# A two-layer fp32 transformer trunk: overlapped halves of the QK projection, layer 1's attention written out, and an earlier first weight split

## What is computed

```
for layer in range(2):
    h = rmsnorm(x, norm_mix[layer])
    if layer == 0:
        q, k, v, u = split(h @ ev_w_in)            # q, k: 2 maps x 4 heads x 64; v: 4 heads x 128
        q, k = rmsnorm(q, q_gain), rmsnorm(k, k_gain)        # over each head's 64
        ya = sub_norm(diff_attention(q, k, v, lam, slopes))  # softmax map 1 - lam * softmax map 2
        yb = multiscale_pool(u)                    # trailing means over 2, 4, 8, 16 tokens
        x = x + concat(ya, yb) @ ev_w_out
    else:
        bg, cg, hc, q, k, v = split(h @ od_w_in)
        yc = bg * conv3(cg * hc)
        q, k = rmsnorm(q, q_gain), rmsnorm(k, k_gain)
        yd = dilated_attention(q, k, v, slopes)    # 8 heads x 64, three (window, dilation) branches
        x = x + concat(yc, yd) @ od_w_out
    x = x + swiglu_ffn(x)                          # width 2816
```

## Time and profile before

| | |
|---|---|
| median of three timed runs | 2280.72 us (2280.49 to 2282.51) |
| the profiled execution's own time | 2289.15 us |
| its span in the trace | 2287.4 us |
| TensorE busy | 2204.0 us (96%), 10600 matmuls |
| VectorE, ScalarE, GpSimd busy | 55%, 39%, 35% |
| chain that ended last, by engine | PE 71%, issue 21%, DVE 4%, ACT 2%, POOL 2% |

### The profile page before, as it was taken

The page is one execution under the profiler, slowest core; times in us unless marked ns, Lnnn a source line. Parts: engine busy times, 40 slices in busy tenths (PEclk is TensorE's granted clock), DMA queues, the critical chain, the costliest instruction groups (busy, mean ns, idle before and its releaser), DMA issues.

```text
span 2287.4 us, 30362 instructions
## 1 busy us (share of the span) xinstructions
PE 2204.0 (96%) x10600; PEld 1840.3 (80%) x10600; DVE 1268.6 (55%) x1771; ACT 884.5 (39%) x1443; POOL 795.8 (35%) x538
## 2 busy tenths in 40 slices
PE   7999897999999999999999998999999999999999
PEld 6876787888888887888888877887888888887887
DVE  4244775676656554558322336566775555554555
ACT  4123874443333333435211126662443333333433
POOL 0022542266666772002000131220367766762000
PEclk9999899999999999999999998999999999999999
DMA  5021120035555547674111111102045555547665
GB/s 178 10 78 28 38 84 19 19 121 192 194 193 167 165 159 272 192 239 137 37 44 48 46 55 38 38 19 74 19 147 194 193 196 164 166 154 267 193 192 194
DMA packets 219222, 283.87 MB, mean 124 GB/s; under 512 B 11504, under 2 KB 120560, under 8 KB 219120
## 3 DMA queue, kind: packets, MB, share of 16 engines
q1 hardware_dynamic: 218832, 282.50, 38.3%
q10 hardware_dynamic: 288, 0.05, 0.0%
HBM read 199.67 MB, written 73.40 MB: 119 GB/s over the span
## 4 chain that ended last, share of the span: by engine, by line
PE 71%; issue 21%; DVE 4%; ACT 2%; POOL 2%; DMA 0%; POOLq 0%; DVEq 0%; SPq 0%; ACTq 0%
PE PS L1284 12%; PE PS L1285 12%; PE PS L1286 12%; PE PS L1311 6%; PE PS L1313 6%; PE PS L1312 6%; PE PS L1007 3%; PE PS L919 3%; PE PS L921 3%; PE PS L920 3%; PE PS L991 2%; POOL QRS L832 1%; PE PS L971 1%; PE PS L972 1%; PE PS L937 1%
## 5 line engine op out<-in xcount | busy, mean ns | idle before, releaser
L1799 DVE TENSOR_TENSOR LINEl<-LINE,HIGH 128x1024 fp32r<-128x1024 f32 x154 | 193.8, 1264 | 170.2 <-ACT HIGH L1342 169.9
L1342 ACT ACTIVATE HIGH<-LINE 128x1024 fp32r<-128x1024 f32 x154 | 162.5, 1059 | 236.6 <-PE PS L1313 232.2
L1311 PE MATMUL PS<-HIGH 128*128 128x512 f32 x616 | 241.8, 393 | 7.0 <-DVE LINEl L1799 7.0
L1312 PE MATMUL PS<-LINEl,HIGH 128*128 128x512 f32 x616 | 240.8, 391 | 0.0
L1313 PE MATMUL PS<-HIGH,LINEl 128*128 128x512 f32 x616 | 240.8, 391 | 0.0
L1799 DVE TENSOR_TENSOR SLOTl<-BLOCKS,RING 128x512 fp32r<-128x512 f32 x168 | 157.7, 939 | 96.8 <-ACT RING L1342 92.0
L807 POOL TENSOR_TENSOR ST<-ST 128x512 f32<-128x512 f32 x132 | 191.9, 1454 | 34.4 <-DMA ST<-in_ffn_w_down 25.7
L1342 ACT ACTIVATE RING<-BLOCKS 128x512 fp32r<-128x512 f32 x168 | 105.9, 631 | 227.7 <-PE PS L1286 223.6
L832 POOL TENSOR_TENSOR QRS<-QMS,EXPO 128x8 f32<-128x8 f32 x32 | 52.0, 1639 | 383.3 <-DVE QMS L1962 383.2
L1799 DVE TENSOR_TENSOR SLOTl<-SLOT,RING 128x512 fp32r<-128x512 f32 x126 | 134.4, 1066 | 86.6 <-ACT RING L1342 86.3
L1311 PEld LDWEIGHTS PS<-HIGH 128*128 128x128 f32 x616 | 116.3, 189 | 32.0 <-DVE LINEl L1799 8.3
(11 more groups left out here) (299 smaller groups left out, 5711.7 us busy)
## 6 DMA issues: line engine op xcount, KB each, us to landing
LINE<-hidden SPq DMA_DIRECT2D x154, 256.0 KB, 2.7
hidden<-HID SPq DMA_DIRECT2D x44, 512.0 KB, 4.4
ST<-in_ffn_w_down SPq DMA_DIRECT2D x44, 512.0 KB, 4.2
sums<-ST SPq DMA_DIRECT2D x22, 1024.0 KB, 6.1
hidden<-ST SPq DMA_DIRECT2D x22, 1024.0 KB, 6.7
LINE<-sums SPq DMA_DIRECT2D x88, 256.0 KB, 3.0
BLOCKS<-in_ffn_w_gate SPq DMA_DIRECT2D x42, 512.0 KB, 4.0
BLOCKS<-in_ffn_w_up SPq DMA_DIRECT2D x42, 512.0 KB, 5.2
```

Source lines behind the costliest of these rows:

```text
L1311: pe.matmul(dst, hi[:, 0, ts], hi[:, 1, :], start=j == 0 and not adds_on, stop=False, skip_group_check=adds_on)
L1312: pe.matmul(dst, hi[:, 0, ts], lo[:, 1, :], start=False, stop=False, skip_group_check=adds_on)
L1342: return nc.scalar.activation(dst, src, ACT.Copy, **kw)
L1799: return v.tensor_tensor(dst, src, hi.bitcast(F32), ALU.subtract)
```

## The change

In four parts:

1. **Start.** The gain is loaded ahead of X tile 1. ScalarE splits the first V half before it makes tile 0's `HH`. Its low part is made in two pieces at once, k = 0, 1 on VectorE ahead of tile 0's `HL`, and k = 2, 3 on GpSimd (a new semaphore `wv_half`), between the second and the third power of the norm. VectorE's constants move behind the split of the second half. TensorE runs 28 transposes of the identity into bank 7 before anything else, and 12 more just before value tile 0; nobody reads them.
2. **QK projection**, both layers. The loop over s is written out, and half 0's turns for t = 5, 6, 7 are issued behind tiles 0, 1, 2 of half 1's first pass.
3. **Layer 1's attention** is written out on the four engines, and nothing of a fifth unit is made; the semaphore targets after it shrink accordingly.
4. **Attention start**, layer 1: VectorE makes unit 0's first two `biased` after six of the eight stack steps.

```
@@ sync: order of the first loads
             load_x(0)
+            gain(0)
             load_x(1)
-            gain(0)
@@ sync: staging of K
-                parts += [(u, stacks_before(L, u) + 2, 0, TOK) for u in range(1, UNITS + L)]
+                parts += [(u, stacks_before(L, u) + 2, 0, TOK) for u in range(1, UNITS)]
@@ gpsimd: norm_power
                     nc.gpsimd.tensor_tensor(RST[:, t:t + 1], MSQ[:, t:t + 1], EXPO[:, 0:1], ALU.pow).then_inc(rs_done, 1)
+                    if n == 0 and t == 1:
+                        pool.wait_ge(rs_done, 2)
+                        pool.wait_ge(wv_hi, 1)
+                        nc.gpsimd.tensor_tensor(WVl[0][:, 2:4, :], RVS[0][0][:, 2:4, :], WVh[0][:, 2:4, :].bitcast(F32),
+                                                ALU.subtract).then_inc(wv_half, 1)
+                        pool.wait_ge(wv_half, 1)
@@ tensor: value_tile and start
+                    if L == 0 and t == 0 and k == 2:
+                        pe.wait_ge(wv_half, 1)
...
+                    for k in range(28):
+                        pe.transpose(bank(7)[:, P * (k % 4):P * (k % 4) + P], IDN[:], IDN[:])
                     for t in range(NT + 2):
+                        if t == 2:
+                            for k in range(12):
+                                pe.transpose(bank(7)[:, P * (k % 4):P * (k % 4) + P], IDN[:], IDN[:])
                         if t >= 2:
                             value_tile(0, t - 2)
@@ tensor: QK projection
-                with pe.Fori(0, 2) as s:
...
+                for s in range(2):
                     for q in range(4):
...
                             if q == 3:
                                 last.then_inc(qk_pe, 1)
                                 if t >= 3:
-                                    qk_turn(t - 3)
+                                    qk_turn(s, t - 3)
+
+                            if s == 1 and q == 0 and t < 3:
+                                qk_turn(0, NT - 3 + t)
                         if q < 3:
                             last.then_inc(wq_pe[L], 1)
-                    for t in range(NT - 3, NT):
-                        qk_turn(t)
+                for t in range(NT - 3, NT):
+                    qk_turn(1, t)
@@ tensor: attention of layer 1 (scalar, vector and gpsimd in the same way)
-                    with pe.Fori(0, 2) as it:
-                        for b in range(2):
-                            u = 2 * it + b
...
+                    for u in range(UNITS):
+                        b, g, h = u % 2, NT * u, 4 * u
+                        following = stacks_before(1, u + 1)
+                        for i in range(NT):
+                            more = u + 1 < UNITS or i < NT - 2
...
+                            if more:
+                                score(1, 0, b, g, i + 2)
+                            turn(1, 1, g, h, i)
+                            weigh(1, 0, u, g, h, i)
+                            if i == NT - 2 and more:
+                                pe.wait_ge(stack_lo, following + 4)
+                            if more:
+                                score(1, 1, b, g, i + 2)
+                            weigh(1, 1, u, g, h, i)
@@ scalar: norm and V of layer 0
                     for t in range(NT + 2):
+                        if t == 2:
+                            split_v(0, 0)
                         if t >= 2:
                             norm_hi(0, t - 2)
                         if t == 2:
-                            split_v(0, 0)
                             split_v(0, 1)
@@ vector: norm and V of layer 0
+                        if t == 2:
+
+                            dve.wait_ge(wv_hi, 1)
+                            low(WVl[0][:, 0:2, :], RVS[0][0][:, 0:2, :], WVh[0][:, 0:2, :]).then_inc(wv_lo, 1)
                         if t >= 2:
                             norm_lo(0, t - 2)
                         if t == 2:
-                            split_v(0)
                             split_v(1)
+                            constants()
@@ vector: attention start
+                for k, step in enumerate(STACK0):
+                    src, hi, lo = stack(step, 0, 0)
+                    if k == 4 and L == 1:
+                        bias(1, 0, 1)
+                    if k == 6 and L == 1:
+                        att.wait()
+                        biased(0, 0, 0, 0)
+                        biased(1, 0, 0, 0)
```

More of the change, by code:

```diff
@@ L887, in _ @@
                 else:
[L888 to L891 removed]
+                    for u in range(1, UNITS):
+                        for k in range(STACKS):
+                            low_stack(k, u % 2, u, stacks_before(1, u) + k)
                 norm_power(2 * L + 1)
@@ L1045, in _, with qk_turn @@
                         columns(WGh[:, s], WGl[:, s], 2 * (j % pairs)).then_inc(ja_pe[L], 1)
[L1047 to L1052 removed]
+                def qk_turn(s, t):
+                    pe.wait_ge(qk_n, 2 * NT * L + NT * s + t + 1)
+                    for j in range(4):
+                        last = pe.transpose(bank(t)[:, P * j:P * j + P], QN[t % 2][:, P * j:P * j + P], IDN[:])
+                    last.then_inc(qk_tp, 1)
+                for s in range(2):
                     for q in range(4):
@@ L2002, in _ @@
                 qk_apply(1, NT - 1)
-                for k, step in enumerate(STACK0):
-                    src, hi, lo = stack(step, 0, 0)
-                    if k == 4 and L == 1:
-                        bias(1, 0, 1)
-                    dve.wait_ge(stack_hi, STACK_AT[L] + k + 1)
-                    if k > 0:
-                        dve.wait_ge(stack_lo, STACK_AT[L] + k)
-                    v.tensor_tensor(lo, src, hi.bitcast(F32), ALU.subtract).then_inc(stack_lo, 1)
-                if L == 0:
-                    for c in (1, 3):
-                        dve.wait_ge(mx_pe, c + 1)
-                        v.tensor_scalar(U[:, c, :], bank(2 * c, 2), PSC[:, c:c + 1], None, ALU.mult).then_inc(mix_ok, 1)
-                per_iter = 2 * (2 + 16)
-                before = att.n
                 def biased(m, b, g, i):
```

175 lines of the change are left out of this document (84 added, 91 removed).

## The result

The changed kernel takes 2264.07 us (median of 4 runs, 2261.71 to 2265.03), the kernel before beside it on the same chip 2281.61 us (2280.49 to 2282.65): a ratio of 0.9918, with a 95% interval of 0.9905 to 0.993. Forecast was 2263.3. The kernel before was run many more times beside the experiments: 46 runs, median 2283.3, from 2279.3 to 2289.9. The changed kernel has 8 runs with a repeat further down, median 2263.4, from 2261.7 to 2265.2. So the best figure for the gain is 19.9 us, a little over the 17.4 of the sum. The spread is smaller too: a standard deviation of 1.3 us over the 8 runs against 2.9 over the 46.

The account below looks back on a forecast made before the run. TensorE, busy nearly all the time, was taken as the bound; only closing idle or shortening half-clock stretches helps. 8.1 + 4.3 + 1.3 + 0.9 + 2.8 = 17.4 us off the 2280.72 median gives 2263.3 us, range 2257 to 2271.

Parts of the forecast that it names:

- QK projection, 8.1 us: Between QK halves, both layers: TensorE's idle time goes, 3.2 us each, plus 1.7 us of half speed in layer 1.
- rival 3: Between QK halves: half 1's tiles wait for weights or banks instead, all 8.1 us lost, 2271.4 us; chance 0.04.
- rival 4: Layer 1's attention: straight code comes too slowly, 3.0 us a wait, with eight waits 2287.3 us; chance 0.05.
- Loop boundary, 4.3 us: Layer 1's attention: written out, unit 2 follows unit 1 in 38.92 us instead of 43.18, saving 4.3 us.
- Fifth unit, 1.3 us: Last unit's tiles 6 and 7, layer 1: without unneeded work the last `weigh` starts sooner, saving 1.3 us (0.6 to 2.2).
- Attention start, 0.9 us: Layer 1's attention start: with `biased` ahead of the last low-part pair, the first `turn` comes 0.9 us sooner; lower end 0.
- Start, 2.8 us: Value tile 0: starts at 15.3 instead of 16.88 and spends less time at half speed, 2.8 us, between 1.5 and 4.3.
- the upper end: Value tile 0: at the higher clock from the beginning it ends at 21.0 instead of 25.3, saving 4.3 us.
- rival 1: Start: the added transposes don't raise the clock, value tile 0 only starts 1.5 us sooner, 2264.6 us; chance 0.2.
- The base: Whole kernel: profiled execution, 2289.15 us, lies 8.43 us above the median 2280.72, a difference taken as the same for both kernels.

Follow-up runs that it names:

- the last two kernels: Changed kernel plus filler identity transposes at layer 1's attention end, with or without 20 more ahead of the first scores: 2261.4 us with, 2260.21 us without.

## Why the prediction was right

The predicted 2263.3 lies 0.8 us under the measured 2264.07, but that is partly two errors against each other. By its own steps:

- **QK projection, 8.1 us.** Right: 3.19 + 4.79 = 7.98 in the first pair of profiles, 4.83 + 3.12 = 7.95 in the repeats, 7.5 alone. The clock's share of 1.7 us was put on layer 1 because one profile had it there. It moves between the layers from profile to profile: the profile of the start alone has it in both (clock 0.66 in 160 to 165 us, 0.57 in 1321 to 1325), those of the attention written out (with and without the fifth unit) in neither. Layer 0's second half is 50.6 us long without the fall, 52.2 with it and 47.4 in every profile with the new order: 3.2 us for the idle time, as the prediction had it, and 1.6 for the clock where it fell. The seven profiles with the old order have seven such falls in their two layers together, on average one a profile. No overlap moved a wait (rival 3), and no engine waited for straight code (rival 4): from 1376 to 1516 us of the changed kernel's profile all waits on issue together are 2.7 us, none over 0.7.
- **Loop boundary, 4.3 us.** This is the step that failed: "Written out, unit 2 should follow unit 1 as unit 1 follows unit 0". The difference of two units of the loop prices only what happens once an iteration. What every unit of the loop pays cancels in it. The repeat of the kernel before would have given 42.12 - 36.91 = 5.2 by the same subtraction, and that too is short. The term was given no upper end above itself, so the range didn't hold it either. The part gave 10.0 to 12.9 us in the traces and 9.4 alone with the fifth unit kept. In the repeats, where the falls are few: 1.1 us for each of three units, 3.3; at the boundary 2.88 us from the loop's jump; these two are 6.2. VectorE's loop alone made 116.85 - 108.53 = 8.3 in the traces, so 2.1 are left. The falls at unit starts took 3.4 us of TensorE's work more in the one (3.4 and 1.7 us) than in the other (1.7): enough to cover them, but not a match. The last 1.7 (108.53 to 106.81) came with the other engines' loops and the last fall. That the falls *follow from* TensorE's idle time is what the profiles suggest (all five with VectorE's loop have one right behind the boundary, with 1.8 to 4.5 us of work lost; of the nine others only the one with VectorE's loop alone written out has one there, 1.7 us), but nothing here changed the idle time alone.
- **Fifth unit, 1.3 us.** Too high: 0.3 in the traces, 0.1 to 0.7 in time. Its work was counted as TensorE's, but the last tiles go at the pace of `weigh`, `scaled` and the next `weigh`, and what lay between had room. In two of the five profiles without it and without fillers (the changed kernel's first, and the one without the 40 transposes) the emptier tiles were followed by a fall of the clock that cost more, 3.4 us of work; in the seven profiles with the fifth unit kept that was not seen, and seven transposes a tile in its place (the last two kernels) also showed none.
- **Attention start, 0.9 us.** Right for the turn, not for what follows: from the last `QN` the turn came 10.43 us later before and 9.69 after, 0.7, in the repeats 10.11 and 9.68, 0.4. But unit 0's first 128x1024 `biased` came 32.3 to 33.8 us after that `QN` in every kernel, with and without this part, as the fall of the clock there went. What hung on it was not the turn alone, and no run shows this part by itself in the time.
- **Start, 2.8 us.** Right in size: 3.4 alone. At tile 2's transposes it is 3.35 in the first pair of profiles and 1.77 in the repeats, because the stretch at half speed is not always 5.7 us: in the seven profiles with the old start these transposes stand at 23.50 to 25.83, on average 24.5, in the five with the new start, its transposes and GpSimd's half at 21.62 to 21.94, on average 21.8. That is 2.7 us, 1.6 of it from the added transposes (23.39 without them). The 2.8 was a choice between 1.5 and 4.3, so that it fits is luck in part. Value tile 0 started at 15.66 where 15.3 was expected; 0.3 of it is `RV`, copied from 11.30 and not from 11.0. The clock was up from the first product, the condition of the upper end; but the tile started 0.4 us later and waited 0.4 for the second half's low part, and the base was lower than 25.3 in most profiles. The time alone doesn't decide this: rival 1's 2264.6 lies as near to the measured 2264.07 as the forecast. The trace does. The Trainium skill's rule ("TensorE: Matmul & The Clock Gate", part 4, PE-mode transpose), by which transposes don't bring the full clock and rival 1 would come true, does not hold here: eight took 1.04 us behind the added ones and 1.94 without them. The Trainium skill also gives, in that section, about 275 ns for one (measured in bf16); with the duration of one the trace agrees, 273 ns in the median at full clock, but back to back they follow each other every 0.13 us (1.04/8), and that is what one costs here.
- **The base.** "A difference I take to be the same for both kernels" was wrong: the profiled execution of before lay 8.4 us above the median, that of the changed kernel 1.0. Sums made against a profiled execution that has more falls of the clock than usual overstate what its stages cost; the median of three runs that the prediction started from, 2280.72, was itself 2.6 below that of 46. So the sum is 2.5 short of the 19.9 us, the loop's term 5.1 or more short with the fifth unit 1.0 and the attention start up to 0.9 too long, and the low base made up for the rest. That the forecast hit so closely is luck.

What stays open: which idle time decides whether the clock falls at a given unit start, what the 3.0 us of TensorE's loop alone are, what makes the larger part of the 1.1 us a unit of VectorE's loop, and whether the 40 transposes are worth anything in time.

## What to carry to other kernels

A loop is priced by what its body costs written out, not by comparing its iterations: the difference between two iterations shows the jump, but not what every iteration pays, here 1.1 us a unit, in part as 0.1 us at each hand-over to an instruction with a register in its address. Look in the chain of waits for sequencer pieces ahead of such instructions, and write out first the loop of the engine that has them there; here one of four engines' loops held nearly all. Where falls of the clock change from run to run, take the base from several profiles, and read a stage's cost from the one with the fewest falls.

## What the runs showed of the hardware that was not expected

- VectorE's jump at a loop's end takes 2.88 us on the chain (3.0 in the waits), TensorE's, ScalarE's and GpSimd's at the same place did not take its place when it went: 11.2 us of the gain are had with their loops still there.
- An instruction of VectorE whose address comes from the loop's register started 0.20 us after the `weigh` it waited for, 0.10 with the loop written out and a constant address.
- Identity transposes alone bring TensorE to 2.4 GHz: 28 from 4.00 us on, the first work of the engine, and the next eight in 1.04 us.
- VectorE's subtraction of 128x2048 took 2.90 us where it met the last 0.75 us of GpSimd's of 128x1024 (3.35 us), 2.28 without it: of the 1.1 us given away, 0.6 came back. Two others of VectorE's, one begun before GpSimd's and one with an input in PSUM, took their usual 1.2 us beside it.
- The same program has its falls of the clock at other places in each execution, and stages with the same code differ by 1.6 us and more for it (50.6 or 52.2 us for layer 0's second QK half). The 46 runs of the kernel before lie 10.5 us apart, the 8 of the changed kernel 3.5.
